# Adaptive-modulation sums placed in other slots of the projection schedule, and two pieces of vector work placed ahead of the product of the second row block

## The chip, the cores and the metric

One core of a Trainium2 chip runs the whole kernel. The metric is the device time of one execution in microseconds; for the kernel before, the median of three runs.

## What is computed

One layer of a hybrid encoder on 256 rows of width 2048, in fp32. Cut to what matters:

```
ada = silu(c) @ w_ada + b_ada                # six vectors of 2048: sh_m, sc_m, gt_m, sh_f, sc_f, gt_f
h   = rms_norm(x) * (1 + sc_m) + sh_m
proj = h @ w_in                              # attention q, k, v; linear attention q, k, v, r
y   = concat(diff_attention(...), gla(...) * silu(rb)) @ w_out
x   = x + gt_m * rms_norm(y)
h   = rms_norm(x) * (1 + sc_f) + sh_f
y   = hier_moe(h)                            # 32 experts, two of them per row
out = x + gt_f * rms_norm(y)
```

`w_ada` is 100 MB, `w_in` 50 MB, `w_out` 17 MB, and the expert weights are 403 MB, so most of the traffic is the experts'.

## The kernel before

Five engines run their own instruction streams, in order, and wait for each other by semaphores. The SP engine issues nearly all weight loads. The streams of all engines in the middle of the program are made from one list, `schedule()`: each engine walks the list and issues its part of each item.

*Beginning.* Vectors 0 and 1 of the modulation are summed in stages, and the first 2048 columns of `w_in` are multiplied beside them.

*Slots.* Then come 32 slots (`SLOTS`). A slot is one `proj` item: sixteen matmul rows in the trace at L706 (or L703), half of a projection block of 256 or 512 columns. The weights come as units of 4 MB in two buffers (`S0`, `S1`), loaded at L494 (`w_in`, units 0 to 7) and L497 (`w_out`, units 8 to 11). Beside the slots stand:

- `("ada", n)`, 64 of them: the modulation vectors 2 to 5 take 16 each (`m = 2 + n // 16`). One is a VectorE pass over 128x2048 that adds a scaled quarter of `w_ada` (1 MB, load at L503) to an accumulator (L1108, for the first of a vector L1106). The loads rotate through four quarter buffers: load n waits on SP until accumulation n - 4 is done. `ADA_AT` holds the slots between which each vector's 16 are spread; `ada_slot(n)` gives the slot.
- `("partial", m)`: the accumulator is turned (L1080) and reduced (L1082) on VectorE; `("mod", m)`: TensorE folds the result over partitions (L607) and VectorE adds the bias (L1112).
- `("att", j)`, from slot 6: one softmax pass of a head and row block on VectorE and ScalarE (L1235 to L1246), its scores on TensorE (L724), the turning of the probabilities (L741) and the product with v (L733). After every fourth pass the head rows are scaled (L1253) and turned (L747, L1257).
- from slot 25 the linear attention: `kv` and `glao` (L766, L758 on TensorE, L1273 and L1275 on VectorE), `silu` and `gmul` (L1264 to L1266, L1285), and the turning `glaT` of its rows (L776).

*Output.* After the slots TensorE does four output products (`wout u t`, L788), column block u of 512, row block t, for the first 1024 columns. ScalarE broadcasts the gain row (`g1b`, L1651) after the second of them, and VectorE multiplies by it (`gain_y`, L1128) at the third, in front of the accumulations there. The other 1024 columns are computed in Strassen's manner from block sums: `mix S` sums the left blocks (four VectorE instructions, L1136), `T1` to `T4` the right blocks (one of 4.4 us each), which need the third and fourth `w_out` units; `prod 0` to `prod 6` are seven products of 1024 deep (L821).

*SP's order.* `loads()` sorts unit loads and ada loads by due slot. Units 9, 10 and 11 wait for the end of the slots, of the second and of the fourth output product. Behind the last of these loads SP waits for accumulation 64 and loads the first expert weights (L507, L510) into a ring of five 4 MB buffers.

*Experts.* Tiles of 32 rows run on TensorE (L915, L969, L876) in a loop; a ring buffer is loaded again when its products are done (L537, L543, L562).

The lines that set the order:

```
        if w == 0:
            out += [("silu", 1, 1), ("gmul", 1, 1), ("partial", 4), ("wout", 0, 0), ("glaT", 1), ("mod", 4)]
        else:
            out.append(("wout", w // 2, w % 2))
        out += [("ada", n) for n in range(48, 64) if ada_slot(n) == SLOTS + w]
```

Of the kernel before, what the change touches and what calls it, by code (L numbers as in the profile page):

```python
# [27 lines left out]
S = 256  # L28
# [42 lines left out]
SLOTS = 32  # L71
FILLS = HELD + SLOTS // 2
ATT_FROM = 6
ADA_AT = [0, 11, 21, SLOTS, SLOTS + 4]

def rows_of(j):
# [26 lines left out]
def slot_unit(s):  # L104

    return 4 + s // 4, s // 2 % 2, s % 2

def ada_slot(n):

    m, k = n // 16, n % 16
    lo, hi = ADA_AT[m:m + 2]
    return lo + k * (hi - lo) // 16
# [36 lines left out]
def schedule():  # L150

    beside = [[] for _ in range(SLOTS)]
    beside[0].append(("alpha", 0))
    beside[1].append(("row",))
    beside[2] += [("alpha", 1), ("lam",)]
    beside[4].append(("alpha", 2))
    beside[5].append(("flip",))
    for m in (2, 3):
        last = ada_slot(KD * (m - 1) - 1)
        beside[last + 1].append(("partial", m))  # L160
        beside[last + 2].append(("mod", m))
    for n in range(48):
        beside[ada_slot(n)].append(("ada", n))
    for j in range(ATT + 3):
        beside[ATT_FROM + j].append(("att", j))
    beside[12].append(("kdec",))
    for j in range(5):
        if j:
            beside[25 + j].append(("glao", j - 1))
        if j < 4:  # L170
            beside[25 + j].append(("kv", j))
    beside[26] += [("silu", 0, 0)]
    beside[28] += [("gsq", 0), ("silu", 1, 0)]
    beside[29] += [("gmul", 0, 0)]
    beside[30] += [("gsq", 1), ("silu", 0, 1), ("gmul", 0, 1)]
    beside[31] += [("gmul", 1, 0), ("glaT", 0)]
    out = []
    for s in range(SLOTS):
        out.append(("proj",) + slot_unit(s))
        out += beside[s]  # L180
    for w in range(4):
        if w == 0:
            out += [("silu", 1, 1), ("gmul", 1, 1), ("partial", 4), ("wout", 0, 0), ("glaT", 1), ("mod", 4)]
        else:
            out.append(("wout", w // 2, w % 2))
        out += [("ada", n) for n in range(48, 64) if ada_slot(n) == SLOTS + w]
    out += [("mix", "S"), ("prod", 0), ("partial", 5), ("mix", "T1"), ("prod", 1), ("mix", "C11"), ("mod", 5), ("mix", "T3"), ("prod", 2),
            ("mix", "T2"), ("prod", 3), ("mix", "T4"), ("prod", 4), ("mix", "U2"), ("prod", 5), ("prod", 6)]
    return out

# [8 lines left out]
def build(nc, a, out):  # L199
    f32, i32, u32 = mybir.dt.float32, mybir.dt.int32, mybir.dt.uint32  # L200
    ALU, ACT, AX = mybir.AluOpType, mybir.ActivationFunctionType, mybir.AxisListType
    SCHED = schedule()
    ctx = ExitStack()
    with ctx:
# [1621 lines left out]
```

## Time and profile before

| | |
|---|---|
| median of three runs | 1509.74 us (1509.57 to 1510.99) |
| profiled execution, its own time | 1507.54 us |
| its span in the profile | 1505.7 us |
| TensorE busy | 1248.7 us, 83% |
| VectorE busy | 771.5 us, 51% |
| ScalarE busy | 207.5 us, 14% |
| moved | 581.93 MB, mean 386 GB/s |
| chain that ended last | DMA 37%, PE 35%, SPq 17%, DVE 8% |

The span is what the profile covers; the execution's own time is a little longer. Busy shares are means over the whole span; slots, output products and experts have different limits and are read apart. In the profile PE is TensorE, DVE VectorE, ACT ScalarE, SP the load queue; "SPq" in a chain is the time that SP took to issue.

### The profile page before, as it was taken

What the parts mean: (1) busy time and instruction counts of PE and PEld (TensorE: products, weight loads), DVE (VectorE), ACT (ScalarE), POOL (GpSimd) and SP (SyncE); (2) the same over time, 40 slices, a digit from 0 to 9 for tenths busy, and PEclk for the clock granted to TensorE, in tenths of its full rate; (3) what the DMA queues carried; (4) which work ended last, traced back from release to release, by engine and by line L of the source; (5) the groups of instructions that cost most, each with busy time, mean ns of one, the idle gap of its engine ahead of it and who ended that gap; (6) DMA issues with size and microseconds to landing.
All of it is one profiled execution on the core that took longest, in us unless ns stands there. A gap on an engine that the chain in (4) does not pass through costs nothing.

```text
span 1505.7 us, 19016 instructions
## 1 busy us (share of the span) xinstructions
PE 1248.7 (83%) x7349; PEld 553.2 (37%) x7350; DVE 771.5 (51%) x1102; ACT 207.5 (14%) x477; POOL 44.2 (3%) x68
## 2 busy tenths in 40 slices
PE   5799999999999798977677766776876779999967
PEld 4688544744444344322122222221221223333322
DVE  5776167877686876534323423332342244655525
ACT  3111132221111022100000000000000001111103
POOL 0001200000000001000000000000000000000010
PEclk9899999999999999989889989889798899999989
DMA  9999978888688969999999999999999999999996
GB/s 354 393 383 383 343 279 333 308 335 325 271 303 339 406 239 397 426 424 424 428 427 424 426 428 428 424 427 427 425 426 429 426 425 427 428 425 424 428 426 268
DMA packets 101668, 581.93 MB, mean 386 GB/s; under 512 B 6680, under 2 KB 31536, under 8 KB 57856
## 3 DMA queue, kind: packets, MB, share of 16 engines
q1 hardware_dynamic: 98752, 572.81, 93.5%
q10 hardware_dynamic: 1664, 6.46, 1.1%
q0 software_dynamic: 1216, 2.17, 0.5%
q8 instruction: 24, 0.39, 0.1%
q14 instruction: 12, 0.10, 0.0%
HBM read 579.29 MB, written 2.13 MB: 386 GB/s over the span
## 4 chain that ended last, share of the span: by engine, by line
DMA 37%; PE 35%; SPq 17%; DVE 8%; issue 1%; ACT 1%; POOL 0%; ACTq 0%; DVEq 0%
DMA stream<-in_w 32%; PE ps L706 11%; SPq L543 6%; PE ps L915 6%; SPq L562 5%; DMA stream<-in_w_ada 5%; PE ps L969 3%; SPq L537 3%; PE ps L631 3%; SPq L478 2%; PE ps L788 2%; PE ps L703 1%; PE ps L876 1%; PE ps L821 1%; DVE wk L1055 1%
## 5 line engine op out<-in xcount | busy, mean ns | idle before, releaser
L915 PE MATMUL ps<-stream,wk 128*32 128x512 f32 x2304 | 321.8, 687 | 132.8 <-DMA stream<-in_w 131.9
L1382 DVE TENSOR_TENSOR acc<-ps,acc 128x2048 f32<-128x2048 f32 x37 | 84.8, 2291 | 431.6 <-PE ps L876 431.6
L915 PEld LDWEIGHTS ps<-stream,wk 128*32 128x32 f32 x2304 | 70.9, 118 | 372.3 <-issue 296.4
L969 PE MATMUL ps<-stream,cst 128*32 128x512 f32 x1152 | 153.2, 660 | 62.7 <-DMA stream<-in_w 62.6
L706 PE MATMUL ps<-stream 128*128 128x512 f32 x448 | 197.5, 594 | 0.3 <-PE ps L631 0.3
L706 PEld LDWEIGHTS ps<-stream 128*128 128x128 f32 x448 | 83.3, 190 | 99.2 <-issue 98.5
L631 PE MATMUL ps<-stream 128*128 128x256 f32 x512 | 117.4, 392 | 1.8 <-ACT stream L1527 1.8
L631 PEld LDWEIGHTS ps<-stream 128*128 128x128 f32 x512 | 100.5, 198 | 16.4 <-issue 1.9
L922 PEld LDWEIGHTS ps<-cst,wk 128*128 128x128 f32 x576 | 70.1, 192 | 62.0 <-issue 62.0
L1055 DVE SCALAR_TENSOR_TENSOR wk<-stream,cc,wk 128x768 f32<-128x768 f32 (+1 forms) x90 | 83.6, 929 | 11.3 <-DMA stream<-in_w_ada 8.6
L876 PE MATMUL ps<-wk,cst 32*128 32x512 f32 x592 | 88.1, 666 | 0.8 <-ACT wk L1698 0.8
L969 PEld LDWEIGHTS ps<-stream,cst 128*32 128x32 f32 x1152 | 33.2, 115 | 146.4 <-DMA stream<-in_w 86.3
L1382 DVE TENSOR_TENSOR wk<-ps,wk 128x2048 f32<-128x2048 f32 x36 | 82.1, 2280 | 0.0
L922 PE MATMUL ps<-cst,wk 128*128 128x32 f32 x576 | 78.1, 279 | 0.0
L1108 DVE SCALAR_TENSOR_TENSOR acc<-stream,cc,acc 128x2048 f32<-128x2048 f32 x30 | 70.5, 2348 | 11.9 <-DMA stream<-in_w_ada 9.9
L870 PE MATMUL ps<-resid,wrs 128*32 128x512 f32 x592 | 70.3, 592 | 0.2 <-DVE wrs L1369 0.2
L788 PE MATMUL ps<-stream 128*128 128x512 f32 x128 | 57.1, 608 | 3.1 <-ACT stream L1637 1.8
L1690 ACT ACTIVATE wk<-ps 128x512 f32<-128x512 f32 x36 | 21.5, 597 | 261.2 <-PE ps L915 261.2
L821 PE MATMUL ps<-stream 128*128 128x512 f32 x112 | 50.6, 612 | 0.4 <-DVE stream L1136 0.4
L1698 ACT ACTIVATE wk<-ps 128x512 f32<-128x512 f32 x36 | 21.5, 597 | 208.5 <-PE ps L969 208.5
L1389 DVE COPY wk<-ps 128x256 f32<-128x256 f32 x74 | 27.9, 419 | 42.7 <-PE ps L870 42.7
L876 PEld LDWEIGHTS ps<-wk,cst 32*128 32x128 f32 x592 | 24.8, 196 | 44.7 <-issue 43.2
(275 smaller groups left out, 1016.7 us busy)
## 6 DMA issues: line engine op xcount, KB each, us to landing
stream<-in_w SPq DMA_DIRECT2D x190, 2048.0 KB, 40.9
stream<-in_w_ada SPq DMA_DIRECT2D x64, 1024.0 KB, 7.0
stream<-in_w_in SPq DMA_DIRECT2D x8, 4096.0 KB, 16.7
stream<-in_w_ada SPq DMA_DIRECT2D x64, 384.0 KB, 10.0
stream<-in_w_out SPq DMA_DIRECT2D x4, 4096.0 KB, 17.3
stream<-in_w_ada SPq DMA_DIRECT2D x16, 512.0 KB, 10.1
stream<-in_w_in SPq DMA_DIRECT2D x4, 2048.0 KB, 13.3
stream<-in_w_in SPq DMA_DIRECT2D x2, 3072.0 KB, 16.2
```

The source lines that it names most:

```text
L543: sp.dma_start(half(ring(r), j), half(w_unit(e, w3), j)).then_inc(ring_in[r % RING][j], 16)
L562: sp.dma_start(half(ring(r), j).rearrange("p (k n) -> p k n", k=2), src[:, 2 * j:2 * j + 2, :]).then_inc(ring_in[r % RING][j], 16)
L631: last = nc.tensor.matmul(bank(u if held else HELD, 2, S)[:, part, :], home(k, k + 1)[:, 0, 256 * u + P * part:256 * u + P * part + P], hT ...
L706: last = nc.tensor.matmul(bank(fill % 2), hT[:, k, P * half:P * half + P], w[:, k, :], start=(k == 0), stop=(k == KD - 1))
L788: last = nc.tensor.matmul(bank(fill % 2), lhs, w[:, k, :], start=(k == 0), stop=(k == KD - 1))
L876: last = nc.tensor.matmul(ps[:, b0 + g, :], spread[32 * g:32 * g + 32, t2, :], ye[32 * g:32 * g + 32, :], start=not onto, stop=True)
L915: last = nc.tensor.matmul(bank(1 + m)[32 * g:32 * g + 32, :], xe[:, k + g, :], w13[m][:, k + g, :], start=(k == 0), stop=(k == KD - 4))
L922: last = nc.tensor.matmul(bank(1 + m, 4, ROWS)[:, c, :], ab[m][:, P * c:P * c + P], cst[:, C_FOLD:C_FOLD + ROWS], start=True, stop=True)
L969: last = nc.tensor.matmul(bank(2)[32 * g:32 * g + 32, :], hid[:, k, :], w2v[:, k, 512 * g:512 * g + 512], start=(k == 0), stop=(k == 3))
L1055: ins = V.scalar_tensor_tensor(out=out_, in0=w, scalar=cc[:, 2, k:k + 1], in1=out_, op0=ALU.mult, op1=ALU.add)
L1108: V.scalar_tensor_tensor(out=acc_m, in0=w, scalar=col, in1=acc_m, op0=ALU.mult, op1=ALU.add).then_inc(ada_done, 1)
L1382: V.tensor_tensor(y4, ps[:, b0:b0 + 4, :], y4, ALU.add).then_inc(ysum_sb, 1)
```

## The change

The table `ADA_AT` becomes 0, 10, 20, 30 and 35: vector 2 is summed in slots 0 to 9, vector 3 in 10 to 19, vector 4 in 20 to 29, and vector 5 in slots 30 and 31 and beside the first three output products, where it stood beside all four. The items `partial` and `mod` of vectors 2 and 3 move one slot ahead. `mix S` stands in front of the (now empty) accumulations of the fourth output product, and `partial 5` in front of `prod 0`.

```
--- before.py
+++ after.py
@@ -71,7 +71,7 @@
 SLOTS = 32
 FILLS = HELD + SLOTS // 2
 ATT_FROM = 6
-ADA_AT = [0, 11, 21, SLOTS, SLOTS + 4]
+ADA_AT = [0, 10, 20, 30, SLOTS + 3]
 
 
 def rows_of(j):
@@ -159,8 +159,9 @@
         last = ada_slot(KD * (m - 1) - 1)
         beside[last + 1].append(("partial", m))
         beside[last + 2].append(("mod", m))
-    for n in range(48):
-        beside[ada_slot(n)].append(("ada", n))
+    for n in range(64):
+        if ada_slot(n) < SLOTS:
+            beside[ada_slot(n)].append(("ada", n))
     for j in range(ATT + 3):
         beside[ATT_FROM + j].append(("att", j))
     beside[12].append(("kdec",))
@@ -183,8 +184,10 @@
             out += [("silu", 1, 1), ("gmul", 1, 1), ("partial", 4), ("wout", 0, 0), ("glaT", 1), ("mod", 4)]
         else:
             out.append(("wout", w // 2, w % 2))
+        if w == 3:
+            out.append(("mix", "S"))
         out += [("ada", n) for n in range(48, 64) if ada_slot(n) == SLOTS + w]
-    out += [("mix", "S"), ("prod", 0), ("partial", 5), ("mix", "T1"), ("prod", 1), ("mix", "C11"), ("mod", 5), ("mix", "T3"), ("prod", 2),
+    out += [("partial", 5), ("prod", 0), ("mix", "T1"), ("prod", 1), ("mix", "C11"), ("mod", 5), ("mix", "T3"), ("prod", 2),
             ("mix", "T2"), ("prod", 3), ("mix", "T4"), ("prod", 4), ("mix", "U2"), ("prod", 5), ("prod", 6)]
     return out
```

The numbers of lines in the changed kernel are 3 higher from `schedule()` on (L1108 is L1111 there).

VectorE at the vector 3 turning: in the order of before it stands behind pass 14 (a pass ends with the two rows at L1245 and L1246; the first line here is the last of that pass).

```order
L1246 SCALAR_TENSOR_TENSOR wk<-wk,st 128x256
L1257 TENSOR_SCALAR stream<-ps,gsub 128x4x128
L1080 STREAM_TRANSPOSE acc<-stream 128x2048
L1082 TENSOR_REDUCE sums<-acc 128x64
L1106 TENSOR_SCALAR acc<-stream,cc 128x2048
L1108 SCALAR_TENSOR_TENSOR acc<-stream,cc,acc 128x2048
L1235 SCALAR_TENSOR_TENSOR wk<-ps,wk 128x512
```

In the changed kernel (`STREAM_TRANSPOSE` and `TENSOR_REDUCE` are the turning, the next two rows the first two accumulations of vector 4) it follows the scaling of the head rows after pass 13:

```order
L1256 TENSOR_TENSOR wk<-ps,st 128x512
L1083 STREAM_TRANSPOSE acc<-stream 128x2048
L1085 TENSOR_REDUCE sums<-acc 128x64
L1109 TENSOR_SCALAR acc<-stream,cc 128x2048
L1111 SCALAR_TENSOR_TENSOR acc<-stream,cc,acc 128x2048
L1238 SCALAR_TENSOR_TENSOR wk<-ps,wk 128x512
```

The turning and the two accumulations moved from ahead of pass 15 to ahead of pass 14.

VectorE from slot 30 to the third output product, before (L1264 to L1266 gate with silu, L1285 multiplies, `wk` is the accumulator of vector 5):

```order
L1108 SCALAR_TENSOR_TENSOR acc<-stream,cc,acc 128x2048
L1285 SCALAR_TENSOR_TENSOR stream<-ps,st,stream 128x256 x2
L1264 TENSOR_SCALAR resid<-resid 128x512
L1265 RECIPROCAL resid<-resid 128x512
L1266 TENSOR_TENSOR stream<-stream,resid 128x512
L1285 SCALAR_TENSOR_TENSOR stream<-ps,st,stream 128x256 x2
L1080 STREAM_TRANSPOSE stream<-acc 128x2048
L1082 TENSOR_REDUCE sums<-stream 128x64
L1112 TENSOR_TENSOR mod<-ps,bada 128x16
L1115 SCALAR_TENSOR_TENSOR mod<-mod,gains 128x16
L1106 TENSOR_SCALAR wk<-stream,cc 128x2048
L1108 SCALAR_TENSOR_TENSOR wk<-stream,cc,wk 128x2048 x7
```

and changed:

```order
L1109 TENSOR_SCALAR wk<-stream,cc 128x2048
L1111 SCALAR_TENSOR_TENSOR wk<-stream,cc,wk 128x2048 x3
L1267 TENSOR_SCALAR resid<-resid 128x512
L1268 RECIPROCAL resid<-resid 128x512
L1269 TENSOR_TENSOR stream<-stream,resid 128x512
L1288 SCALAR_TENSOR_TENSOR stream<-ps,st,stream 128x256 x2
L1111 SCALAR_TENSOR_TENSOR wk<-stream,cc,wk 128x2048 x3
L1288 SCALAR_TENSOR_TENSOR stream<-ps,st,stream 128x256 x2
L1267 TENSOR_SCALAR resid<-resid 128x512
L1268 RECIPROCAL resid<-resid 128x512
L1269 TENSOR_TENSOR stream<-stream,resid 128x512
L1288 SCALAR_TENSOR_TENSOR stream<-ps,st,stream 128x256 x2
```

Two accumulations of vector 4 in slots 30 and 31 have become seven of vector 5 (1 + 3 + 3), all ahead of the turning of vector 4. Behind that turning, the eight at the first two output products (L1106 and seven) have become six (L1111, x6).

SP, the loads of this stretch, before:

```order
L497 DMA stream<-in_w_out 128x16x512
L503 DMA stream<-in_w_ada 128x2048 x5
L497 DMA stream<-in_w_out 128x16x512
L503 DMA stream<-in_w_ada 128x2048 x8
L497 DMA stream<-in_w_out 128x16x512
L503 DMA stream<-in_w_ada 128x2048 x4
L497 DMA stream<-in_w_out 128x16x512
```

and changed:

```order
L500 DMA stream<-in_w_out 128x16x512
L506 DMA stream<-in_w_ada 128x2048 x10
L500 DMA stream<-in_w_out 128x16x512
L506 DMA stream<-in_w_ada 128x2048 x5
L500 DMA stream<-in_w_out 128x16x512 x2
```

The second `w_out` unit stands behind ten ada loads instead of five, and the fourth directly behind the third.

## Rows read from the trace of the kernel before

**Rows 1.** the page, part 2: GB/s in each of the 40 slices

```profile
GB/s 354 393 383 383 343 279 333 308 335 325 271 303 339 406 239 397 426 424 424 428 427 424 426 428 428 424 427 427 425 426 429 426 425 427 428 425 424 428 426 268
```

**Rows 2.** transfers between 584 and 1490 us, in sum

```profile
DMA packets 34439, 383.66 MB, mean 423 GB/s; under 512 B 2976, under 2 KB 2976, under 8 KB 2976
```

**Rows 3.** the chain of waits, 405 to 560 us: start us, us, what

```profile
425.86 13.93 PE ps L706 x32
...
441.98 13.99 PE ps L788 x32
...
458.82 15.71 PE ps L788 x32
...
525.50 4.44 DVE stream L1136
...
535.93 4.44 DVE stream L1136
...
540.50 19.55 PE ps L821 x45
```

**Rows 4.** VectorE in order of time: start us, us, what, count [idle before]

```profile
416.96 1.66 DVE L1275 SCALAR_TENSOR_TENSOR resid<-resid,st,ps 128x256 f32<-128x256 f32 x4 [6.81 <-PE ps L758]
...
423.11 4.80 DVE L1108 SCALAR_TENSOR_TENSOR acc<-stream,cc,acc 128x2048 f32<-128x2048 f32 x2
...
442.43 0.43 DVE L1264 TENSOR_SCALAR resid<-resid 128x512 f32<-128x512 f32 x1 [3.01 <-ACT resid L1623]
...
447.87 3.65 DVE L1080 STREAM_TRANSPOSE stream<-acc 128x2048 f32<-128x2048 f32 x1
...
458.98 17.08 DVE L1108 SCALAR_TENSOR_TENSOR wk<-stream,cc,wk 128x2048 f32<-128x2048 f32 x7
...
491.29 1.42 DVE L1128 TENSOR_TENSOR stream<-stream,acc 128x512 f32<-128x512 f32 x2 [12.34 <-DMA acc<-gdram]
...
513.05 5.00 DVE L1136 TENSOR_TENSOR stream<-stream 128x1024 f32<-128x1024 f32 x4
```

**Rows 5.** TensorE in order of time, 471 to 600 us

```profile
501.96 13.98 PE L821 MATMUL ps<-stream 128*128 128x512 f32 x32
524.06 0.31 PE L607 MATMUL ps<-sums,cst 128*32 128x16 f32 x8 [8.12 <-DVE sums L1082]
...
584.65 3.64 PE L915 MATMUL ps<-stream,wk 128*32 128x512 f32 x32 [0.73 <-DVE wk L1395]
```

**Rows 6.** SP's issues in order of time, 380 to 600 us

```profile
381.10 25.45 SPq L503 DMA_DIRECT2D stream<-in_w_ada  x4
406.59 0.43 SPq L497 DMA_DIRECT2D stream<-in_w_out  x1
410.18 28.82 SPq L503 DMA_DIRECT2D stream<-in_w_ada  x5
...
502.86 0.43 SPq L497 DMA_DIRECT2D stream<-in_w_out  x1
```

**Rows 7.** issue to landing: L497 loads issued at 406.59 and at 502.86

```profile
DMA to landing us min/median/max: 15.5/15.5/15.5
...
DMA to landing us min/median/max: 18.7/18.7/18.7
```

**Rows 8.** VectorE in order of time, around the turning of vector 3

```profile
339.68 0.69 DVE L1253 TENSOR_TENSOR wk<-ps,st 128x512 f32<-128x512 f32 x1 [1.56 <-POOL st L1742]
...
346.96 3.64 DVE L1080 STREAM_TRANSPOSE acc<-stream 128x2048 f32<-128x2048 f32 x1
...
356.62 0.68 DVE L1235 SCALAR_TENSOR_TENSOR wk<-ps,wk 128x512 f32<-128x512 f32 x1
```

**Rows 9.** TensorE in order of time, slots 22 and 23

```profile
351.44 7.03 PE L706 MATMUL ps<-stream 128*128 128x512 f32 x16
...
360.50 0.44 PE L741 MATMUL ps<-cst,wk 128*128 128x128 f32 x2 [1.20 <-DVE wk L1246]
```

**Rows 10.** windows, 460 to 465 us: busy by engine, granted clock, DMA share, GB/s

```profile
460.00:465.00 5.00, 5.00 (x10) 2.10 (x9) 4.79 (x3) 0.00 (x0) 0.00 (x0) 0.69 0.92 369
```

More of the change, by code:

```diff
@@ L73 @@
 ATT_FROM = 6
-ADA_AT = [0, 11, 21, SLOTS, SLOTS + 4]
+ADA_AT = [0, 10, 20, 30, SLOTS + 3]
 def rows_of(j):
@@ L161, in schedule @@
         beside[last + 2].append(("mod", m))
-    for n in range(48):
-        beside[ada_slot(n)].append(("ada", n))
+    for n in range(64):
+        if ada_slot(n) < SLOTS:
+            beside[ada_slot(n)].append(("ada", n))
     for j in range(ATT + 3):
@@ L185, in schedule @@
             out.append(("wout", w // 2, w % 2))
+        if w == 3:
+            out.append(("mix", "S"))
         out += [("ada", n) for n in range(48, 64) if ada_slot(n) == SLOTS + w]
-    out += [("mix", "S"), ("prod", 0), ("partial", 5), ("mix", "T1"), ("prod", 1), ("mix", "C11"), ("mod", 5), ("mix", "T3"), ("prod", 2),
+    out += [("partial", 5), ("prod", 0), ("mix", "T1"), ("prod", 1), ("mix", "C11"), ("mod", 5), ("mix", "T3"), ("prod", 2),
             ("mix", "T2"), ("prod", 3), ("mix", "T4"), ("prod", 4), ("mix", "U2"), ("prod", 5), ("prod", 6)]
```

## The prediction

> **What bounds the kernel now.** I first read the slices of the page. From slice 15 on the core moves 424 to 428 GB/s, slice after slice [rows 1], and between 584 us and 1490 us it moves 383.66 MB at a mean of 423 GB/s [rows 2]. The expert part is thus a fixed amount of transfer at a full rate; it begins when TensorE starts the first expert at 584.65 [rows 5] and frees the first ring buffers. An edit ahead of it is worth what it moves that start by, one for one. Slice 14 (527 to 565 us) reaches only 239 GB/s [rows 1]: there the ring loads wait for the products of the second row block, and these wait for VectorE.
>
> So I next read the chain of waits there [rows 3]. It runs through two output products on TensorE (to 474.5), then the broadcast of the gain row (in at 491.2 [rows 4]), the modulation sums of the last vector, their turning, then the block sums, and from 540.50 the last three products. VectorE's timeline shows why [rows 4]: it does seven accumulations in 17.08 us, waits 12.34 us for the gain row, multiplies at 491.29, does eight more accumulations, then the left block sums (`S`) at 513.05 for 5.0 us, then the turning, and only at 525.50 the first right block sum `T1` [rows 3]. TensorE had finished the second half product at 515.9 and stood 8.12 us [rows 5]. `T1` started without waiting for anything: the fourth w_out block, issued 502.86 [rows 6], was in at 521.6 (18.7 us later [rows 7]). The end that counts is that of `T2`, 535.93 + 4.44 = 540.4; the product after it begins 0.1 us later [rows 3].
>
> **What the change does behind the gain row.** Eight accumulations there become three. Five go away, at 17.08 / 7 = 2.44 us each [rows 4]: 12.2 us. `S` and the turning stay ahead of `T1`, so they cost the same; that they now stand ahead of product 0 in the list changes nothing on TensorE, whose own order there stays. VectorE could thus start `T1` about 12 us earlier, near 513, if all before it stayed. What is late next: the fourth w_out block. It is issued when the fourth output product ends, and nothing in the change moves that earlier. Its landing becomes the bound.
>
> **Its landing time.** Before, it took 18.7 us, with accumulation loads still streaming in ahead of it. Now all 64 of these loads are out of the way, and only the first expert load comes behind it. The first w_out block took 15.5 us [rows 7]; it was issued at 406.59, right after an accumulation load (the last of the four of 381.10 to 406.55) [rows 6], so 1.05 MB went ahead, 2.5 us at 423 GB/s [rows 2]. Alone: 13.0 us. I take 13.0, since now the queue is empty; the bounds are 18.7 (as before) and 13.0. The Trainium skill, page "DMA: Bandwidth & Descriptors", section "Anatomy of one DMA", gives about 2.0 us plus bytes over 436 GB/s, measured on another issuing path; for 4.19 MB an estimate of 11.6 us, by which the gain would be 1.4 us larger. The row is 1.4 us above it, and I keep the row.
>
> **What the change costs before.** The five accumulations, and two more, now lie earlier, where VectorE feeds TensorE. I go place by place.
>
> Slots 0 to 19: VectorE runs one or two accumulations ahead of before. It fills waits that it had; the first softmax pass waits for TensorE in many slots. Turning of vector 2 moves from before pass 5 to before pass 4, into such a wait. I take 0; above, about 2 us if pass 4 comes late.
>
> Slots 20 to 23: the turning of vector 3 and two accumulations took from 346.96 to 356.62, 9.66 us, ahead of pass 15; TensorE waited 1.20 us and went on at 360.50, 3.9 us after that pass began [rows 8, 9]. Now this block stands ahead of pass 14. It can start when the head rows are scaled, 339.68 + 0.7 = 340.3 [rows 8], so pass 14 starts near 350.0 and TensorE goes on near 353.9, instead of at 351.44 [rows 9]. That is 2.5 us. The next pass follows after two accumulations in time for a stall that replaces the old 1.20 us, so the slip stays about 2.5.
>
> Slots 24 to 29: one accumulation more or less in a slot; VectorE waited 6.81 us for TensorE before the last state update at 416.96 [rows 4]. Cover is ample: 0.
>
> Slots 30 and 31: seven accumulations instead of two, and here nothing covers them. With the slip the state update comes at 419.5. Up to 423.11 in the old count took 6.15 us [rows 4], so 425.6; one accumulation and a gated product (3.2) give 428.8; four accumulations (the first is a plain multiply, 1.4, then three of 2.44) 437.5; gating and product 5.4, 442.9. TensorE ends its projections at 439.8 + 2.5 = 442.3 [rows 3] and waits 0.6 for the rows that it is to turn. Three accumulations, a product (8.1): 451.0; the last gating and product, as from 442.43 to 447.87, 5.4: 456.4; turning of vector 4 (447.87 + 3.65 + 2.3 = 6.0) 462.4. TensorE, which has to fold that turning ahead of the second output product, goes on at about 462.8. Before it went on at 458.82 [rows 3]. Total slip of the output products: **4.0 us**.
>
> The w_out loads. The second one now stands on SP behind the loads of accumulations up to 58, thus behind the 54th: issued near 450.2 instead of just after 439.0 [rows 6], in by 466, needed at 462.8 + 15.7 = 478.5. Hidden by 12 us. The third waits for the second output product as before.
>
> **The sum.** The fourth block lands at 502.86 + 4.0 + 13.0 = 519.9. VectorE: the gain row, asked for right after the second output product, at 491.2 + 4.0 = 495.2; products 1.4, three accumulations 7.3, `S` 5.0, turning 6.0, products 1.4: ready at 516.4. So `T1` starts at 519.9 instead of 525.50. From there to the end of `T2` it was 14.9 us, the same work: 534.8. TensorE ends product 1 at 519.9 and, at 7 us each, would be ready for that product at 534.2. It starts it at 534.9, 5.6 us earlier than at 540.50. Routing, first expert and the ring loads follow by semaphores and shift with it. **Gain 5.6 us.** The profiled execution had a span of 1505.7 us and took 1507.54 us; the median is 1509.74, 2.2 above it. A shift of 5.6 taken from the median gives 1504.1.
>
> 0.2% is 3.0 us, about the least that a measurement of this kernel tells from no change.
>
> **Rivals.** (a) *The fourth block lands no sooner.* The first expert load, 4.2 MB, now follows it within a microsecond, where before it came 10 us later. If they share the engines, 18.7 us stay: gain 22.64 - 18.7 - 4.0, with 525.50 - 502.86 = 22.64, near 0, so 1509.7. Against it: the first w_out block had an accumulation load 3.6 us behind it (410.18) [rows 6] and still took 15.5. Half such an effect gives 1506.9. Chance 0.20, "no change".
>
> (b) *Slower: the bunch waits for its loads.* Accumulations 48 to 54 rotate through four quarter buffers, and each wait goes straight to the left block, the turning and the second output product. A load is asked for 7.3 us before its use; one that queues behind a w_out load takes at least its 15.5 us [rows 7], a wait of about 8.2 to 8.5. One such wait makes the slip 12.5; a late pass at slots 10 and 11 (the 2 us above) makes it 14.5. What the bunch gives is 22.64 - 13.0 = 9.6, so that is a loss of 4.9, time 1514.6. It decides from a total slip of 9.6 us (loss begins) or 12.6 us (over 0.2%). For: slots 30 and 31 have no cover. Against: the first w_out load is issued near 406 and in by 422, the second only after the bunch. Chance 0.14.
>
 The 8.12 us wait [rows 5] goes away, and with it what the clock lost there, but TensorE was not the bound there. Chance 0.12.
>
> (d) *The slip is smaller.* With none, `T1` is bound by a landing at 515.9: gain 9.6, 1500.1. Chance 0.08.
>
> **How the numbers follow.** My forecast (gain 3.3 to 8) has 0.46. Faster by over 0.2%: 0.46 + 0.12 + 0.08 = 0.66. Within 0.2%: 0.20. Slower: 0.14. The range goes from (d), 1500.1, to just past (a), 1510.5, and leaves out most of (b).
>
> **What would show it.** VectorE's wait for the gain row followed by three accumulations, not eight; `T1` ended by a wait for the w_out block, landing 13 to 14 us after issue; TensorE waiting 2 to 3 us near 352 and again until near 462 for sums; output products 4 us later; product 4 and the first expert about 5 to 6 us earlier; the rate of slice 16 and on unchanged. A landing near 18 us, waits of VectorE for in_w_ada between 429 and 451, or output products over 9 us late would make it wrong.

## The result and the profile after

| | before | changed |
|---|---|---|
| median of five runs | 1509.74 us (1508.21 to 1510.99) | 1501.46 us (1501.20 to 1502.87) |
| ratio, 95% interval | | 0.9944 (0.9932 to 0.9957) |
| profiled execution, its own time | 1507.54 us | 1502.87 us |
| its span | 1505.7 us | 1501.0 us |
| TensorE busy | 1248.7 us, 83% | 1246.9 us, 83% |
| VectorE busy | 771.5 us, 51% | 772.2 us, 51% |
| moved | 581.93 MB, mean 386 GB/s | 581.93 MB, mean 388 GB/s |

The change is 8.3 us faster by the medians; by the interval of the ratio, 6.5 to 10.3 us. One run of the changed kernel took twice as long and one of a later version (vector 5 over four products) a third longer; ranges and ratios leave them out, and without the first the changed kernel's median is 1501.43 us.

The work is the same, and so is the amount moved. What differs is where the transfer engines stand idle. The slices of the page, part 2, GB/s in each of 40:

```profile
GB/s 354 393 383 385 368 261 361 307 337 304 295 321 382 306 292 395 427 423 426 428 426 424 428 426 425 425 429 426 425 427 427 426 425 428 426 426 425 427 426 262
```

From slice 16 on the row is that of before [rows 1] within a few GB/s. Slice 14 rose from 239 to 292: the ring loads of the experts come earlier (the first is issued at 507.32, before at 513.16).

TensorE in order of time, 350 to 360 us and 440 to 580 us of the changed kernel (start, length, line, shapes, count, and in brackets the idle time before and what ended it; its line numbers are 3 higher than before's):

```profile
354.75 0.44 PE L744 MATMUL ps<-cst,wk 128*128 128x128 f32 x2 [1.80 <-DVE wk L1249]
355.03 8.73 PE L709 MATMUL ps<-stream 128*128 128x512 f32 x16
...
444.21 1.09 PE L779 MATMUL ps<-cst,stream 128*128 128x128 f32 x8 [0.85 <-DVE stream L1288]
446.58 13.97 PE L791 MATMUL ps<-stream 128*128 128x512 f32 x32 [1.27 <-issue]
460.38 1.04 PE L779 MATMUL ps<-cst,stream 128*128 128x128 f32 x8
463.51 0.26 PE L610 MATMUL ps<-sums,cst 128*32 128x16 f32 x8 [2.09 <-DVE sums L1085]
463.70 43.16 PE L791 MATMUL ps<-stream 128*128 128x512 f32 x96
...
506.84 13.98 PE L824 MATMUL ps<-stream 128*128 128x512 f32 x32
520.75 0.26 PE L610 MATMUL ps<-sums,cst 128*32 128x16 f32 x8
520.94 14.00 PE L824 MATMUL ps<-stream 128*128 128x512 f32 x32
535.15 20.84 PE L824 MATMUL ps<-stream 128*128 128x512 f32 x48 [0.21 <-DVE stream L1139]
...
579.33 3.64 PE L918 MATMUL ps<-stream,wk 128*32 128x512 f32 x32 [0.73 <-DVE wk L1398]
```

The 8.12 us wait [rows 5] for the last vector's turning is gone, and so is nearly all idle time between 463.7 and 556. In exchange TensorE waits 1.80 us ahead of slot 22, 0.85 for a left block's rows, and reaches the second output product later. The first expert starts at 579.33; before it was 584.65 [rows 5].

VectorE in order of time, same kernel:

```profile
341.18 3.67 DVE L1083 STREAM_TRANSPOSE acc<-stream 128x2048 f32<-128x2048 f32 x1
...
350.86 0.68 DVE L1238 SCALAR_TENSOR_TENSOR wk<-ps,wk 128x512 f32<-128x512 f32 x1
...
457.46 3.67 DVE L1083 STREAM_TRANSPOSE stream<-acc 128x2048 f32<-128x2048 f32 x1
...
464.33 14.63 DVE L1111 SCALAR_TENSOR_TENSOR wk<-stream,cc,wk 128x2048 f32<-128x2048 f32 x6
...
494.58 1.42 DVE L1131 TENSOR_TENSOR stream<-stream,acc 128x512 f32<-128x512 f32 x2 [12.73 <-ACT stream L1647]
496.04 7.26 DVE L1111 SCALAR_TENSOR_TENSOR wk<-stream,cc,wk 128x2048 f32<-128x2048 f32 x3
503.21 5.00 DVE L1139 TENSOR_TENSOR stream<-stream 128x1024 f32<-128x1024 f32 x4
508.25 3.65 DVE L1083 STREAM_TRANSPOSE stream<-wk 128x2048 f32<-128x2048 f32 x1
...
514.25 1.42 DVE L1131 TENSOR_TENSOR stream<-stream,acc 128x512 f32<-128x512 f32 x2
520.14 4.43 DVE L1139 TENSOR_TENSOR stream<-stream 128x4096 f32<-128x4096 f32 x1 [4.48 <-DMA stream<-in_w_out]
```

Three accumulations stand behind the gain row, not eight. The last row is `T1`: VectorE was ready at 515.7 and waited 4.48 us for the fourth `w_out` block. The chain of waits of the changed kernel says the same:

```profile
463.77 43.11 PE ps L791 x96
506.90 13.17 DMA stream<-in_w_out
...
520.14 4.44 DVE stream L1139
...
530.58 4.44 DVE stream L1139
...
535.15 20.85 PE ps L824 x48
```

Where before the chain went over the gain row, sums and block sums [rows 3], it now goes straight from the fourth output product over one load to `T1`.

**Where the time came from.** Executions differ in when slot 0 starts (163.50 us before, 165.04 in this one, 164.4 to 166.9 elsewhere, for either order) and in how long the expert part takes (920.9 to 923.9 us), neither of which the change touches. So I count from the start of slot 0 to the first expert in each profile: 421.15 us before, 414.29 changed, 6.9 us less. I use this measure below, beside the medians:

| from slot 0's start, us | before | changed |
|---|---|---|
| output product 1 | 278.48 | 281.54 |
| output product 2 | 295.32 | 298.66 |
| product 0 | 338.46 | 341.80 |
| fourth `w_out` load issued | 339.36 | 341.86 |
| `T1` | 362.00 | 355.10 |
| first expert | 421.15 | 414.29 |

### The profile page after: what moved, and what is told of

It is laid out like the page before. It is cut to its first block, busy times and chain, and to the rows that moved or that the text cites. A ratio compares the mean times of both kernels' runs of the same rounds, so it can differ in the third digit from the quotient of the medians.

```text
span 1501.0 us, 19016 instructions
## 1 busy us (share of the span) xinstructions
PE 1246.9 (83%) x7349; PEld 552.2 (37%) x7350; DVE 772.2 (51%) x1102; ACT 207.4 (14%) x477; POOL 45.4 (3%) x68
## 2 busy tenths in 40 slices
DMA packets 101668, 581.93 MB, mean 388 GB/s; under 512 B 6680, under 2 KB 31536, under 8 KB 57856
## 4 chain that ended last, share of the span: by engine, by line
PE 38%; DMA 35%; SPq 16%; DVE 9%; issue 1%; ACT 1%; POOL 0%; ACTq 0%; DVEq 0%
DMA stream<-in_w 32%; PE ps L709 10%; PE ps L918 6%; PE ps L634 5%; SPq L546 5%; SPq L565 4%; SPq L540 4%; PE ps L972 3%; PE ps L791 3%; DMA stream<-in_w_ada 2%; DVE wk L1058 2%; PE ps L879 2%; PE ps L706 1%; PE ps L824 1%; PE ps L925 1%
## 5 line engine op out<-in xcount | busy, mean ns | idle before, releaser
L1111 DVE SCALAR_TENSOR_TENSOR acc<-stream,cc,acc 128x2048 f32<-128x2048 f32 x30 | 70.5, 2350 | 11.9 <-DMA stream<-in_w_ada 9.6
```

The source lines that it names most:

```text
L1111: V.scalar_tensor_tensor(out=acc_m, in0=w, scalar=col, in1=acc_m, op0=ALU.mult, op1=ALU.add).then_inc(ada_done, 1)
```

## Experiments

After the result two readings were open. *Theory A:* behind the fourth output product the landing of the fourth `w_out` block bounds `T1`, with about 4.5 us of slack on VectorE, and the 3.3 us of slip ahead of it is the price of the crowded slots. *Theory B:* VectorE's shorter work behind the gain row is the gain, whatever is done in the slots, and nothing stands close behind VectorE. "Expert" is the time from slot 0's start to the first expert.

### Fewer sums behind the gain row, without the early slots

Before, with one edit: the 16 sums of vector 5 beside three output products instead of four.

```
-ADA_AT = [0, 11, 21, SLOTS, SLOTS + 4]
+ADA_AT = [0, 11, 21, SLOTS, SLOTS + 3]
```

> The kernel before with one number changed: vector 5 ends beside the third output product (6, 5 and 5 accumulations beside the first three), nothing moves into the slots. Landing theory (T1 starts when the fourth w_out block is in, and this depends on how much was queued ahead): the same bytes are asked for after 458 us as before, the transfer engines were full from 465 us on, so the block still lands near 521.5; T1 starts there instead of 525.5: gain about 4 us, time near 1505.7, VectorE idle before T1 on the w_out block. Rival (only VectorE's work behind the gain row counts): three accumulations fewer there, ready near 517.5: gain about 8 us, near 1501.7. No slip of the output products in either.

Measured: 1510.56 us, ratio 1.0003 (0.9994 to 1.0012); expert 421.21, as before to 0.1 us. VectorE of this kernel, 495 to 530 us:

```profile
495.78 1.42 DVE L1128 TENSOR_TENSOR stream<-stream,acc 128x512 f32<-128x512 f32 x2 [7.73 <-DMA acc<-gdram]
497.24 9.71 DVE L1108 SCALAR_TENSOR_TENSOR wk<-stream,cc,wk 128x2048 f32<-128x2048 f32 x4
512.45 2.35 DVE L1108 SCALAR_TENSOR_TENSOR wk<-stream,cc,wk 128x2048 f32<-128x2048 f32 x1 [5.50 <-DMA stream<-in_w_ada]
...
527.23 4.42 DVE L1136 TENSOR_TENSOR stream<-stream 128x4096 f32<-128x4096 f32 x1
```

SP's issues and TensorE of the same kernel:

```profile
460.61 24.89 SPq L503 DMA_DIRECT2D stream<-in_w_ada  x11
485.55 0.43 SPq L497 DMA_DIRECT2D stream<-in_w_out  x1
```

```profile
509.99 16.89 PE L821 MATMUL ps<-stream 128*128 128x512 f32 x32 [6.13 <-DMA stream<-in_w_out]
```

And its windows (busy us of PE, PEld, DVE, ACT, POOL with counts; granted clock; DMA share; GB/s):

```profile
480.00:490.00 10.00, 10.00 (x25) 4.50 (x24) 7.80 (x6) 0.00 (x0) 0.00 (x0) 1.00 1.01 422
490.00:500.00 10.00, 10.00 (x24) 4.37 (x24) 4.05 (x4) 1.28 (x3) 0.00 (x0) 1.00 1.01 408
500.00:510.00 10.00, 3.87 (x12) 1.72 (x10) 6.74 (x3) 1.28 (x3) 0.00 (x0) 0.95 1.05 396
```

Both expectations missed. The bunch ahead of the gain row grew to eleven. SP issues in order, and the loads of that bunch wait for accumulations, so the third `w_out` load went out 320.36 us after slot 0's start; before it was 312.96, in the change 314.39. It took 24.4 us, no longer than before (24.4; in the change 21.6), so its later issue is what made product 0 wait 6.13 us. On VectorE the 7.3 us of the three accumulations went into a gain row that came 2.8 us later (330.59 after slot 0's start, before 327.79) and into the 5.50 us wait of the last accumulation, whose load SP had put behind the third `w_out` load. The fourth block took 19.5 us and landed 358.05 us after slot 0's start; before it landed at 358.06. The landing theory was right in this, and wrong in that VectorE would be ready: `T1` started at 362.04 and waited for nothing.

Three accumulations fewer behind the gain row were worth nothing: the same bytes went through engines that were full (a share of 1.00 or more in every 10 us from 470 to 520, before too), and VectorE's last sum had to wait for its share of them. What the change does in slots 0 to 31 takes seven sums and their 7.3 MB out of this stretch (nine accumulations behind 460 us instead of sixteen); with it the shorter tail gains, without it nothing. Whether the room in the transfers or the earlier place of the third load on SP counts for more is not shown: no run moves only one of them. In the change the engines are empty when the fourth block is asked for (windows of the changed kernel):

```profile
500.00:505.00 5.00, 5.00 (x13) 2.13 (x13) 4.86 (x4) 0.00 (x0) 0.00 (x0) 1.00 0.01 2
```

### Only the order of the left block and the turning

Before, with the left block sums in front of the accumulations of the fourth output product and `partial 5` in front of `prod 0`; `ADA_AT` as before.

```
+        if w == 3:
+            out.append(("mix", "S"))
         out += [("ada", n) for n in range(48, 64) if ada_slot(n) == SLOTS + w]
-    out += [("mix", "S"), ("prod", 0), ("partial", 5), ("mix", "T1"),
+    out += [("partial", 5), ("prod", 0), ("mix", "T1"),
```

> The kernel before with only the other part of the change: the left block sums ahead of the last four accumulations, the turning named ahead of product 0. VectorE does the same work before T1. Both theories: gain 0, time near 1509.7 (within 1 us), T1 near 525.5. If it gained by itself more than 3 us, the place of the left block sums would matter, which my account denies.

Measured: 1508.32 us, ratio 0.9992 (0.9982 to 1.0001); expert 420.22, 0.9 less than before. VectorE does the same work in another order and reaches `T1` 361.0 us after slot 0, not 362.0. Before, an accumulation at 503.33 waited 0.87 us for its load; here the left block sums stand in that place, and no accumulation waits. In the order of before, this part of the change is worth about a microsecond; the medians do not tell it from none.

### How much slack VectorE has: 3.65 and 7.3 us more work ahead of T1

The changed kernel with the turning of vector 5 done twice, or three times, into the same place (the result is the same).

```
+                if m == 5:
+                    for _ in range(1):          # 2 in the second kernel
+                        link(V.transpose(turn..., acc_of(m)...))
```

> The changed kernel with the transpose of vector 5 done twice (3.65 us more on VectorE just before T1). Landing theory: VectorE waited 4.48 us for the fourth w_out block, so this hides: same time as the changed kernel within 0.5 us, about 8 us faster than the kernel before. Rival (VectorE's work bounds): 3.65 us slower than the changed kernel.

> The changed kernel with that transpose done three times (7.3 us more). Landing theory: 4.48 us hidden, the rest not: T1 about 2.8 us later than in the changed kernel, time 2.8 us above it, 5 to 5.5 us faster than the kernel before. Rival (VectorE's work bounds throughout): 7.3 us above the changed kernel, so about 1 us faster than the kernel before.

Measured: with one more, 1501.69 us, ratio 0.9947 (0.9934 to 0.9961); `T1` at 354.98 after slot 0, where the change has 355.10. 3.65 us of added work cost nothing, and the wait for the load shrank from 4.48 to 0.52 us:

```profile
519.34 4.42 DVE L1142 TENSOR_TENSOR stream<-stream 128x4096 f32<-128x4096 f32 x1 [0.52 <-DMA stream<-in_w_out]
```

With two more, 1508.98 us, ratio 0.9986 (0.9976 to 0.9997): 7.5 us slower than the change by the medians, 4.8 by the expert time (419.12), where 2.8 was expected. The median alone would fit the rival's 7.3; the kernel with one more turning, 3.65 us slower by the rival, does not. `T1` started without a wait, 3.1 us later. TensorE of this kernel:

```profile
522.07 0.26 PE L610 MATMUL ps<-sums,cst 128*32 128x16 f32 x8 [1.04 <-DVE sums L1088]
...
538.51 22.54 PE L824 MATMUL ps<-stream 128*128 128x512 f32 x48 [2.25 <-DVE stream L1142]
```

3.1 us of the 4.8 is `T1`'s delay, 1.7 the last products, 22.54 us instead of 20.84: the windows show a granted clock of 0.69 between the 2.4 and 1.2 GHz levels in 540 to 545 us, after the 2.25 us wait. Theory A holds in the traces: the landing ends `T1`'s wait, with 4.5 us to spare on VectorE, and what goes beyond them moves `T1`. Of what the medians show beyond the 4.8, this profile has 0.9 in the expert part (922.61 us against 921.67) and 0.2 in the start; the other 1.5 us are not explained.

### The slip: vectors 2 and 3 put back

The changed kernel, with vectors 2 and 3 spread as before and only vectors 4 and 5 moved.

```
-ADA_AT = [0, 10, 20, 30, SLOTS + 3]
+ADA_AT = [0, 11, 21, 30, SLOTS + 3]
```

> The changed kernel with vectors 2 and 3 back in their old slots (0 to 10 and 11 to 20), vector 4 in 21 to 29, vector 5 from 30 on as in the change. Slip theory (what the early turning of vector 3 costs goes one for one into the end): the wait of TensorE at the end of slot 21 and the slower slot after it (8.56 us instead of 6.87) go away, 1.2 us of wait at slot 22 comes back: output products 2.3 us earlier, first expert 2.3 us earlier, time near 1499.2. Rival (VectorE's load in slots 21 to 29 is now too dense and makes a wait of the same size): same as the changed kernel or slower, 1501 to 1504.

Measured: 1500.14 us, ratio 0.9932 (0.9919 to 0.9945). Expert 408.90, 5.4 less than the changed kernel. Since profiles scatter, it was run again on one chip with before and the change:

> The kernel before, unchanged, once more, for its own spread. Ratio 1.000 within 0.1%. From slot 0 to the first expert 420 to 421.5 us, as in the three profiles with its order of work; start of slot 0 anywhere from 163 to 167 us and the expert part anywhere from 921 to 924 us, which I hold to be differences between executions and not between kernels. If slot 0 or the expert part came out on one side for this order and on the other for the changed one, part of the measured gain would come from there.

> The changed kernel once more. Theory (everything is won between slot 0 and the first expert, 6 to 7 us): ratio 0.9955, that is 6.8 us, within its interval; profile from slot 0 to first expert 413 to 415 us. Rival (the expert part is shorter too, by about 1.5 us): ratio 0.9944 again, and an expert part under 921.5 us.

> Vectors 2 and 3 in their old slots, vectors 4 and 5 as in the change, once more, beside the changed kernel on one chip. Slip theory: 2.3 us faster than the changed kernel (the wait at slot 21 and the slow slot behind it), 1 to 3.5 us being its scatter; TensorE's wait ahead of slot 22 absent. Rival (no difference): within 0.5 us of the changed kernel.

| on one chip | median | ratio to before, interval | output product 1 | product 0 | first expert |
|---|---|---|---|---|---|
| before | 1510.88 | 1.0003 (0.9994 to 1.0012) | 278.46 | 338.43 | 421.10 |
| changed | 1503.81 | 0.9962 (0.9948 to 0.9976) | 281.51 | 341.75 | 414.47 |
| vectors 2 and 3 back | 1499.98 | 0.9935 (0.9922 to 0.9949) | 279.49 | 338.03 | 410.57 |

(The three columns on the right count from slot 0's start. The ratios are to all runs of before of that batch, median 1510.43.) This version beats both kernels: 3.8 us faster than the change by the medians, 3.9 by the expert time, more than the 2.3 expected, and its slowest run (1500.95) is below the change's fastest (1503.73). TensorE of it at slots 22 and 23:

```profile
353.47 7.03 PE L709 MATMUL ps<-stream 128*128 128x512 f32 x16
...
362.53 0.44 PE L744 MATMUL ps<-cst,wk 128*128 128x128 f32 x2 [1.20 <-DVE wk L1249]
```

The 1.80 us wait ahead of slot 22 is gone, the 1.20 of before [rows 9] is back, and slot 22 takes 7.03 us again, not 8.73. That is 2.0 us at output product 1. The other 1.7 us come at output product 2, where the three products took 41.47 us, not 43.16: in this execution the clock did not fall there, though the wait in front of them was as long (2.06 us). The first execution of this version had the same 41.47 us, and both of before and both of the change a fall, so it repeats; nothing here says why. In that first execution output product 1 came 3.7 us earlier than in the change, not 2.0; 1.1 of the difference lies in slot 13, which took 7.07 us there and 8.17 in the second execution:

```profile
279.10 7.07 PE L706 MATMUL ps<-stream 128*128 128x256 f32 x32
```

```profile
278.30 8.17 PE L706 MATMUL ps<-stream 128*128 128x256 f32 x32
```

The early turning of vector 3 was thus the costly part of the slip, with 2.0 us or more of the 3.3. Vector 2 was put back with it, but nothing was lost before: in the change slot 21 begins 179.36 us after slot 0's start, in the order of before at 179.57.

### One sum less in slots 30 and 31

The changed kernel with vector 5 spread over all four output products again.

```
-ADA_AT = [0, 10, 20, 30, SLOTS + 3]
+ADA_AT = [0, 10, 20, 30, SLOTS + 4]
```

> The changed kernel with vector 5 spread to the fourth output product again (3 and 3 accumulations in slots 30 and 31, 2, 3, 3 and 2 beside the output products), so six instead of seven ahead of the turning of vector 4 and five instead of three behind the gain row. Slip theory: TensorE's wait of 0.85 us for the left block goes, output products about 1.1 us earlier; VectorE ready for T1 2.44 * 2 - 1.1 = 3.8 us later than in the changed kernel, within 0.5 us of the fourth w_out block's landing: net gain 0.6 to 1.1 us, near 1500.6. Rival (the work behind the gain row bounds): 3 to 4 us slower than the changed kernel.

Measured: 1501.81 us, ratio 0.9940 (0.9927 to 0.9953), no different from the change by the medians; the rival's 3 to 4 us slower did not come. The expert time is 2.6 us less. TensorE:

```profile
462.13 0.26 PE L610 MATMUL ps<-sums,cst 128*32 128x16 f32 x8 [0.27 <-DVE sums L1085]
463.85 41.47 PE L791 MATMUL ps<-stream 128*128 128x512 f32 x96 [1.46 <-ACT stream L1640]
```

The 0.85 wait went. The 2.09 us wait for the fold also went, but a wait of 1.46 for ScalarE's eviction of the turned rows took its place; before it was 1.80. So most of the fold's wait costs nothing: it covers a wait that is there anyway. Output product 1 came 1.0 us earlier and output product 2 1.3, as expected; the three products then took 41.47 us, not 43.16, and that 1.7, a clock that did not fall here, is the larger part of the gain. VectorE, now with two sums behind the left block, started `T1` at 352.5 after slot 0 without any wait.

### The landing in two halves

The changed kernel with the fourth `w_out` block as two loads of 2 MB on one queue; `T1` waits for the first, `T3` for the second.

```
-    sp.dma_start(unit_w(i), ...).then_inc(unit_in[i % 2], 16)
+    sp.dma_start(unit_w(i)[:, 0:8, :], ...).then_inc(c_in, 16)
+    sp.dma_start(unit_w(i)[:, 8:16, :], ...).then_inc(unit_in[i % 2], 16)
...
-    dve.wait_ge(unit_in[1], 16 * 6)
+    dve.wait_ge(c_in, 32)
```

> The changed kernel with the fourth w_out block loaded as two transfers of 2 MB, T1 waiting for the first alone and T3 for the second. Landing theory: T1 starts near 515.7 to 516 instead of 520.1, as soon as VectorE is ready; T2 ends 4 us earlier, near 531; but TensorE has five products of 7 us from the second half's landing on, so the product after T2 starts at about 534.1 instead of 535.15: gain 1.0 us over the changed kernel, near 1500.5. Were VectorE's chain the only bound, the gain would be 4.4 us, near 1497. Were the landing not T1's bound, no gain and T1 unmoved.

Measured: 1503.72 us, ratio 0.9954 (0.9941 to 0.9967), no gain over the change (1.0 was expected). The halves landed 8.1 and 13.1 us after their issues. `T1` started 4.4 us earlier, at once when VectorE was ready, but the expert came only 0.5 us earlier:

```profile
517.27 4.42 DVE L1143 TENSOR_TENSOR stream<-stream 128x4096 f32<-128x4096 f32 x1
```

```profile
508.30 13.98 PE L828 MATMUL ps<-stream 128*128 128x512 f32 x32
...
522.40 34.60 PE L828 MATMUL ps<-stream 128*128 128x512 f32 x80
```

From 508.30 on TensorE works its products back to back. In the change the load's landing costs 0.21 us of idle time there and a little at the edges; behind it stands TensorE itself. Thus the landing, which the chain of waits names, is worth 0.5 us, and the slip, which stands in front of it, is worth its whole length.

### Both together

Vectors 2 and 3 back, vector 5 over four products, and the two halves.

> All three together: ADA_AT 0, 11, 21, 30, 36 and the fourth w_out block in two transfers. If the parts add: 2.3 + 1.0 + 1.0, near 1497.2, first expert 4 us earlier than in the changed kernel. If the landing of the fourth block or TensorE's products take back what the slip gives, 1498 to 1500.

Measured: 1500.52 us, ratio 0.9939 (0.9926 to 0.9952); expert 411.35. Both expectations, 1497.2 and 1498 to 1500, were missed. `T1` at 518.33 again without a wait, the product behind it 0.67 us late. The slip is gone: output product 1 comes 278.46 us after slot 0's start and output product 2 at 295.30, both as before. But the clock fell at the latter:

```profile
461.43 43.16 PE L795 MATMUL ps<-stream 128*128 128x512 f32 x96 [1.46 <-ACT stream L1645]
```

This is 1.7 us more than the 41.47 in both profiles with vectors 2 and 3 back, and the granted clock was 0.70 in 460 to 465 us. The time is no better than with vectors 2 and 3 back alone; how much of that is the fall, and how much is that the parts remove the same few microseconds, was not separated.

## Why the prediction was right

It gave 1504.1 us, 1500.1 to 1510.5, and faster; measured were 1501.46 and, beside before on one chip, 1503.81. The mechanism came as forecast; two of its terms were off. Step by step:

- **The rate of the expert part.** Right, with a small misreading: the row at 424 GB/s and more begins with slice 16, not 15, which is 397 [rows 1]. Nothing in the sum hangs on it.
- **The five accumulations off.** Right. Three stand there, VectorE was ready at 515.7; predicted was 516.4.
- **The fourth block as next bound.** Right, `T1` waited 4.48 us for it. It landed in 13.2 us (13.17 in the chain, 13.4 in the second execution), predicted 13.0; before it was 18.7 [rows 7]. The row of the first block was a better guide than that of the fourth, because no other load was in flight (2 GB/s in 500 to 505 us). The Trainium skill, page "DMA: Bandwidth & Descriptors", section "Anatomy of one DMA", by whose figures, measured on another issuing path, the estimate was 11.6, is 1.6 us below the runs here; the measurement decides.
- **The second `w_out` block.** Right: issued 451.73, in 15.4 us later at 467.1, 10 us and more ahead of its need. Between 300 and 470 us VectorE stands idle ahead of an accumulation only twice, 0.46 us each: rival (b) did not come about.
- **Turning of vector 3.** Mechanism right. It ended a wait of 1.80 us ahead of slot 22, and the old 1.20 went away. The slip of 2.5 was predicted as wait alone; it came as 0.6 of wait and 1.70 of slower matmuls, 8.73 instead of 7.03 us, together 2.3 (2.0 at slot 23, since slot 21 had begun 0.2 earlier). The window 355 to 360 us has a granted clock of 0.66. This is the fall that rival (c) spoke of, though it stands inside the size that was forecast, since the wait was smaller. Before, no fall stands behind the 1.20 us wait: granted clock 1.00 in 360 to 365.
- **Slots 30 and 31.** Predicted a 0.6 us wait for the left block; measured 0.85. Predicted the second output product 4.0 later; measured 3.34 (298.66 less 295.32). The term that was too large is the turning of vector 4: the fold waits 2.09 us, but before, TensorE already stood 1.80 us there for ScalarE, and the gap from the rows that it turned to the second output product grew from 3.03 us (455.79 to 458.82) to 3.32 (460.38 to 463.70), 0.3 and not 0.9.
- **The load's issue.** This is the term that failed, by 0.84 us, and the text did not see it: "issued 502.86" plus 4.0. Before, the fourth load was not issued when product 0 began (501.96) but 0.9 us later, behind four `in_w_ada` loads on SP whose last waited for an accumulation (issues from 495.12 to 502.81). In the change nothing stands there, and the load goes out 0.06 us after product 0 begins (506.84 and 506.90). So of 3.34 us slip only 2.50 reach the load.
- **The sum.** From slot 0, `T1` moved by 339.36 + 22.64 - (341.86 + 13.24) = 6.9 us; predicted 5.6. The difference is 1.5 of slip less (0.66 and 0.84) against 0.24 of longer landing. The first expert moved by the same 6.9. The medians show 8.3 in the first comparison; in the second 7.1 against the before kernel on the same chip (1510.88 to 1503.81), and 5.7 by the ratio 0.9962. They lie on both sides of 6.9, and scatter of starts and of the expert part is large enough for that; that it is all of it was not shown.
- **Rivals.** (a) would have needed a landing of 18.7: absent, though the first expert load follows 0.4 us behind. (c) is half there: one new fall at slot 22, the old one at output product 2 stays (43.16 us for three products, in both), none after the 8.12 us wait, since it is gone. (d), no slip, was priced at a gain of 9.6; the version of the last experiment (its load split too), with product 0 at 338.44 after slot 0's start as before, has an expert time 9.8 us below before's.

**What stays open.** What decides whether the clock falls after a wait. A wait of about 2.1 us ahead of output product 2 was followed by 43.16 us in the change and by 41.47 us with vectors 2 and 3 back. A wait of 1.46 us there was followed by 41.47 us in one version and by 43.16 in another. With one more turning it fell in output product 1 instead (15.67 us), and the three after it took 41.47. No version was run to force or forbid a fall.

## What to carry to other kernels

When a wait is shortened, name what is next on each engine and how far off it is: here VectorE had 4.5 us of slack to the load, and the load only 0.5 us to TensorE, so splitting the load gave nothing, and putting vectors 2 and 3 back, ahead of it, gave 3.9 us. Work taken from a late, crowded stretch must take its transfers with it and land where its engine has cover: fewer sums behind the gain row gave 0 us without the early slots and 6.9 with them. Moving vectors 2 and 3 too was not needed for it and cost 2 to 4 us. In an in-order load queue look at what each large load stands behind: in the first experiment small loads that wait for late accumulations held a 4 MB one back for 7.4 us, and the next small one came late behind it.

## What the runs showed of the hardware

- **Short waits and the clock.** The wait of 1.80 us ahead of slot 22 stands in all six profiles with vectors 2 and 3 moved, and the slot took 8.46 to 8.73 us in each; the other seven have 1.20 to 1.24 us ahead of slot 23 instead, and both slots took 7.03. A wait of 1.80 us ahead of output product 2 (four profiles) was followed by 43.16 us for the three products, one of 2.25 by 22.54 for the last products. The windows behind these waits have a granted clock of 0.66, 0.69 and 0.69, and each fall costs 1.7 us of matmul time. But the wait's length alone does not decide. Ahead of output product 2, waits of 2.07 to 2.09 us were followed by 43.16 us in four profiles, and waits of 2.06 and 2.07 by 41.47 in the two with vectors 2 and 3 back; a wait of 1.46 was followed once by each; and in one profile output product 1 took 15.67 us, not 13.97, behind waits of only 0.85 and 1.27. Slot 13, after a wait of 3.34 or 3.35 us a little before it, took 8.17 us in one execution and 7.07 in another of the same kernel. TensorE's wait of 6.13 us in the first experiment was followed by 16.89 us for the two products that take 13.98, with the clock at 0.50, the 1.2 GHz level, in 510 to 515 us.
- **A 4 MB load has several prices.** 13.2 to 13.4 us with nothing in flight; 15.2 to 15.8 with a 1 MB load ahead of it; 18.7 to 24.4 us with more beside or ahead of it (19.5 and 24.4 at a DMA share of 1.01 to 1.05). Two loads of 2 MB, one behind the other, landed 8.1 and 13.1 us after their issues 0.4 us apart: the first comes 5 us ahead of the whole, and the second about when the whole block would.
- **Scatter between executions** of the start (163.50 to 166.93 us at slot 0) and of the expert part (920.9 to 923.9 us) is as large as half the gain of this change. Counting between two landmarks of one profile leaves these two out, but not the clock's falls, 1.1 to 1.7 us each.
